# Delta rule: inverses woven with half projections and operands, output rows reordered; up and gate products with a 512-wide operand

## What is computed

```python
def squared_relu_mlp(h, w_up, w_down):          # hidden 4096, two layers, first one for both sequences
    return jnp.square(jax.nn.relu(h @ w_up)) @ w_down

def _swiglu(h, w_in, w_out):                    # hidden 2816, twice
    gu = h @ w_in
    return (jax.nn.silu(gu[..., :FFN_HIDDEN]) * gu[..., FFN_HIDDEN:]) @ w_out

def _gated_deltanet(h, w_in, conv_w, a_log, dt_bias, norm_w, w_out):
    proj = h @ w_in
    qkv = jax.nn.silu(_causal_depthwise_conv(proj[..., :n_qkv], conv_w))
    z = proj[..., n_qkv:n_qkv + GDN_V_WIDTH].reshape(b, s, GDN_HEADS, GDN_DV)
    ...
    o = _chunk_gated_delta_rule(q, k, v, g, beta)
    o = o * lax.rsqrt(jnp.mean(o * o, axis=-1, keepdims=True) + RMS_EPS)
    o = o * norm_w.astype(jnp.float32) * jax.nn.silu(z.astype(jnp.float32))
    return o.astype(h.dtype).reshape(b, s, GDN_V_WIDTH) @ w_out

def _chunk_gated_delta_rule(q, k, v, g, beta):
    a_mat = jnp.where(strict, kk * beta[..., :, None] * decay, 0.0) + jnp.eye(c, dtype=jnp.float32)
    sol = lax.linalg.triangular_solve(a_mat, rhs, left_side=True, lower=True, unit_diagonal=True)
    ...
```

## Time and profile before

| | |
|---|---|
| median of 3 runs | 2090.27 us (2086.32 to 2092.71) |
| profiled execution | 2091.75 us, span 2089.9 us |
| TensorE busy | 1898.4 us (91%), 12225 products |
| VectorE busy | 1118.6 us (54%) |
| ScalarE busy | 914.0 us (44%) |
| GpSimd busy | 346.9 us (17%) |
| HBM traffic | 153 GB/s over the span |
| mean granted TensorE clock | 0.941 of full speed |

### The profile page before, as it was taken

The page is one execution under the profiler, slowest core; times in us unless marked ns, Lnnn a source line. Parts: engine busy times, 40 slices in busy tenths (PEclk is TensorE's granted clock), DMA queues, the critical chain, the costliest instruction groups (busy, mean ns, idle before and its releaser), DMA issues.

```text
span 2089.9 us, 29077 instructions
## 1 busy us (share of the span) xinstructions
PE 1898.4 (91%) x12225; PEld 1636.4 (78%) x12225; DVE 1118.6 (54%) x1555; ACT 914.0 (44%) x1419; POOL 346.9 (17%) x396
## 2 busy tenths in 40 slices
PE   4879887999999999968799989998799999999999
PEld 2666656888887887756598969898699978768997
DVE  1555556555575544566455557833445455565554
ACT  2543344344455444634354447532344344444443
POOL 2120112211141121120211130130200005200000
PEclk8899988999999999989899989998999999999999
DMA  8353553445555766421645544310355545504553
GB/s 278 126 201 126 196 178 109 152 146 189 188 170 182 241 212 227 128 82 39 189 151 193 183 142 132 108 64 1 106 170 179 181 167 175 177 1 141 182 190 133
DMA packets 217966, 320.61 MB, mean 153 GB/s; under 512 B 8550, under 2 KB 123946, under 8 KB 217452
## 3 DMA queue, kind: packets, MB, share of 16 engines
q1 hardware_dynamic: 212628, 308.96, 45.5%
q0 software_dynamic: 1744, 6.03, 0.8%
q10 hardware_dynamic: 3464, 3.75, 0.6%
HBM read 317.68 MB, written 1.05 MB: 153 GB/s over the span
## 4 chain that ended last, share of the span: by engine, by line
PE 77%; DVE 9%; ACT 6%; DMA 4%; POOL 2%; issue 2%; SPq 0%; POOLq 0%; ACTq 0%; DVEq 0%
PE ps L69 74%; PE ps L77 3%; DVE WLO L86 3%; DMA RAW<-in_w_mod_dram 1%; ACT WHI L80 1%; DMA RAW<-in_w_in_dram 1%; DVE AR L86 1%; ACT AR L80 1%; POOL SM L86 1%; DMA RAW<-in_w_up_dram 1%; DVE SM L99 1%; ACT XR L80 1%; DVE PMD L86 1%; POOL XR L86 1%; ACT PMD L80 1%
## 5 line engine op out<-in xcount | busy, mean ns | idle before, releaser
L86 DVE TENSOR_TENSOR WLO<-RAW,WHI 128x1024 fp32r<-128x1024 f32 (+2 forms) x504 | 593.6, 1219 | 430.0 <-ACT WHI L80 429.9
L80 ACT ACTIVATE WHI<-RAW 128x1024 fp32r<-128x1024 f32 (+2 forms) x504 | 488.1, 1017 | 416.2 <-PE ps L69 305.6
L69 PE MATMUL ps<-TH,WHI 128*128 128x256 f32 x1664 | 481.6, 289 | 13.2 <-DVE TL L86 10.9
L69 PE MATMUL ps<-TL,WHI 128*128 128x256 f32 x1664 | 476.9, 287 | 0.0
L69 PE MATMUL ps<-TH,WLO 128*128 128x256 f32 x1664 | 476.4, 286 | 0.0
L69 PE MATMUL ps<-WHI,ARR 128*128 128x512 f32 x1120 | 355.8, 394 | 6.1 <-DVE ARR L86 3.1
L69 PEld LDWEIGHTS ps<-TH,WHI 128*128 128x128 f32 x1664 | 325.6, 196 | 23.9 <-issue 13.5
L69 PEld LDWEIGHTS ps<-TL,WHI 128*128 128x128 f32 x1664 | 325.8, 196 | 0.2
L69 PEld LDWEIGHTS ps<-TH,WLO 128*128 128x128 f32 x1664 | 325.5, 196 | 0.0
L69 PE MATMUL ps<-WHI,TH 128*128 128x512 f32 (+2 forms) x608 | 240.9, 396 | 23.3 <-DVE WLO L86 22.7
L69 PEld LDWEIGHTS ps<-WHI,ARR 128*128 128x128 f32 x1120 | 211.0, 188 | 57.2 <-issue 9.3
(11 more groups left out here) (193 smaller groups left out, 1957.1 us busy)
## 6 DMA issues: line engine op xcount, KB each, us to landing
RAW<-in_w_mod_dram SPq DMA_DIRECT2D x48, 1024.0 KB, 5.3
RAW<-in_w_up_dram SPq DMA_DIRECT2D x48, 1024.0 KB, 5.4
RAW<-in_w_down_dram SPq DMA_DIRECT2D x48, 1024.0 KB, 5.2
RAW<-in_ffn_w_in_dram SPq DMA_DIRECT2D x44, 1024.0 KB, 5.1
RAW<-in_w_in_dram SPq DMA_DIRECT2D x20, 1024.0 KB, 5.3
RAW<-in_ffn_w_out_dram SPq DMA_DIRECT2D x20, 1024.0 KB, 5.1
RAW<-in_dil_w_in_dram SPq DMA_DIRECT2D x18, 1024.0 KB, 5.1
RAW<-in_gdn_w_in_dram SPq DMA_DIRECT2D x16, 1024.0 KB, 5.6
```

The source lines that it names most:

```text
L69: return Made(None if self.eng is None else self.eng.matmul(o, l, r, start=start, stop=stop))
L80: return Made(None if self.eng is None else self.eng.activation(o, i, f, **k))
L86: return Made(None if self.eng is None else self.eng.tensor_tensor(o, a, b, op))
```

## The change

- A product of a half now has one PSUM bank of its own. The moving operand of the high weights is TH and TL together (T2, one tensor TT, two runs of 256 tokens), 512 wide, into both halves of the bank; the low weights with TH go 256 wide into the first half. VectorE then adds the halves (`dve_halves`), a reduction over pairs 256 numbers apart, into SBUF. Relu and Silu now run in place in SBUF. In the feedforward the product of gate and up goes from VectorE to GpSimd (`pool_ffn`) and is rounded one pair later. The convolution projections keep their old form, but hand out a step for each half.
- In the delta rule the convolutions from the eighth on (ALONE = 7) count as two steps each; q's normalisation runs beside the last four, and the operand steps beside the gate's z units from the third. The weave is now 20 steps with 20.
- In the chunks `ring` gets banks 5, 6, 7, 2, 3, 4; outputs 2 and 3 come before the transposes of 0 and 1; GpSimd gates two groups at a time. `pe_gdnout` goes through the first column half token tile by token tile, tile 2 ahead of the transposes of groups 2 and 3; the second weight tile is split before them.

```diff
-        def pe_cols_half(t, b, f, xh, xl, cs, need):
+        def pe_cols_half(key, t, f, nt, cs, need):
             hi, lo = t.of(t.hi), t.of(t.lo)
-            o = b[:, 256 * f:256 * f + 256]
+            fs = slice(128 * f, 128 * f + 128)
+            x2 = T2v(nt)
+            banks.take((key, f), gring)
+            wait_free((key, f))
+            b = banks.of((key, f))
+            both, first = b.rearrange("p (s t) -> p s t", s=2), b[:, 0:256]
             for k in range(8):
                 pe.wait_ge(dve_w, ("lo", t.i, k // 4))
                 need(k)
-                m = pe.matmul3(o, hi[:, k, 128 * f:128 * f + 128], lo[:, k, 128 * f:128 * f + 128], xh[:, k, cs], xl[:, k, cs], k == 0, k == 7)
-            return m
+                if k > 0:
+                    pe.matmul(first, lo[:, k, fs], x2[:, 0, k, cs], False, False)
+                m = pe.matmul(both, hi[:, k, fs], x2[:, :, k, cs], k == 0, k == 7)
+                if k == 0:
+                    pe.matmul(first, lo[:, k, fs], x2[:, 0, k, cs], False, False)
+            m.then_inc(pe_gemm, ("acc", key, f), *([("used", t.i)] if f == 1 else []))
+
+        def dve_halves(signal, o, key, f, *said):
+            b = banks.of((key, f))
+            dve.wait_ge(pe_gemm, ("acc", key, f))
+            dve.reduce(o, b.rearrange("p (s t) -> p t s", s=2), ALU.add).then_inc(signal, ("free", (key, f)), *said)
...
+        def dve_upsum(l, sq, hc, c, f):
+            key, _, _ = up_parts(l, sq, hc, c)
+            wait_tmp(dve, l, sq, key)
+            dve_halves(dve_hd, tmp(l, sq, key)[:, 256 * f:256 * f + 256], ("up", l, sq, hc, c), f, ("sum", key, f))
...
         def pe_rest():
+            qn, ops = pe_l2(0), pe_operands()
             for n, c in enumerate(CONVS):
-                pe_conv(c)
+                for f, _ in enumerate(pe_conv(c)):
+                    if n >= ALONE:
+                        if n > ALONE:
+                            next(qn, None)
+                        yield
...
+            run(qn)
             for c in range(2):
-                for _ in pe_rows(("z", c), z_spec(c), TLS, rows_of("gdn"), normed("gdn")):
-                    next(qn, None)
+                for i, _ in enumerate(pe_rows(("z", c), z_spec(c), TLS, rows_of("gdn"), normed("gdn"))):
+                    if 4 * c + i >= 2:
+                        next(ops)
                     yield
-            yield from qn
-            yield from pe_operands()
+            yield from ops
...
         def pe_chunks():
+            ring.set(5, 6, 7, 2, 3, 4)
+            gring.set(0, 1, 2, 3)
...
             pe_value(3)
+            pe_output(2)
+            pe_output(3)
             pe_outturn(0)
-            pe_output(2)
             pe_outturn(1)
-            pe_output(3)
+
+        def pe_gdnout():
+            g = pe_rows(("go", 0), GDN_OUT[0], TLS, gdn_lhs, gdn_need, apart=True)
+            advance(g, 2)
             pe_outturn(2)
             pe_outturn(3)
+            run(g)
+            run(pe_rows(("go", 1), GDN_OUT[1], TLS, gdn_lhs, gdn_need))
...
-            weave((rest, 22), (inv, 20))
+            weave((rest, 20), (inv, 20))
...
         def act_ffn(l, t):
+            def rounded(c):
+                _, tb, hi, _ = ffn_parts(c)
+                act.wait_ge(pool_hd, ("fm", l, c))
+                act.act(hi, tb, ACT.Copy).then_inc(act_hd, ("fh", l, c))
             for c in range(11):
+                ta = ffn_parts(c)[0]
                 act_splits(tile_of["ffn_w_in_2", l, 0, 256 * c])
+                if c >= 1:
+                    rounded(c - 1)
+                act.wait_ge(dve_hd, ("sum", l, c, 0, 1))
+                act.act(ta, ta, ACT.Silu).then_inc(act_hd, ("fs", l, c))
                 act_splits(tile_of["ffn_w_in_2", l, 0, FFH + 256 * c])
...
         def dve_ffn(l, t):
+            def rest(c):
+                _, tb, hi, lo = ffn_parts(c)
+                dve.wait_ge(act_hd, ("fh", l, c))
+                dve.tt(lo, tb, hi.bitcast(F32), ALU.subtract).then_inc(dve_hd, ("f", l, c))
             for c in range(11):
+                for x, o in enumerate(ffn_parts(c)[0:2]):
+                    dve_splits(tile_of["ffn_w_in_2", l, 0, FFH * x + 256 * c])
+                    if c >= 1 and x == 0:
+                        rest(c - 1)
+                    if c >= 4:
+                        dve.wait_ge(*((pool_hd, ("fm", l, c - 4)) if x == 0 else (dve_hd, ("f", l, c - 4))))
+                    for f in range(2):
+                        dve_halves(dve_hd, o[:, 256 * f:256 * f + 256], ("f", l, c, x), f, ("sum", l, c, x, f))
+            rest(10)
```

More of the change, by code:

```diff
@@ L403, in spec, with row_steps, pe_rows @@
             return [(name, idx, k, min(4, k0 + nk - k), c0, n) for k in range(k0, k0 + nk, 4)]
-        def pe_rows(key, ws, tls, lhs, need, r=gring):
+        def row_steps(ws, tls, apart):
+            steps = [((c, w), ti) for c, w in enumerate(ws) for ti in tls]
+            return sorted(steps, key=lambda s: s[1]) if apart else steps
+        def pe_rows(key, ws, tls, lhs, need, r=gring, apart=False):
             n, nk = ws[0][5], sum(w[3] for w in ws)
-            for c, w in enumerate(ws):
+            for (c, w), ti in row_steps(ws, tls, apart):
@@ new lines, in pe_rows @@
+                o = banks.of((key, ti))[:, 0:n]
+                for k in range(t.nk):
+                    kk = t.k0 - ws[0][2] + k
+                    pe.wait_ge(dve_w, ("lo", t.i, 2 * k // t.nk))
+                    need(kk, ti)
+                    lh, ll = lhs(kk, ti)
+                    m = pe.matmul3(o, lh, ll, hi[:, k, :], lo[:, k, :], kk == 0, kk == nk - 1)
+                said = [("used", t.i)] if ti == tls[-1] else []
+                if c == len(ws) - 1:
+                    said.append(("acc", key, ti))
@@ L2085, in second @@
                 act_square(t, ti, 1, 7)
-            run(act_rows((gkey, 0), specs[0], TLS, first if t else None))
+            run(act_rows((gkey, 0), specs[0], TLS, first if t else None, apart))
             run(act_rows((gkey, 1), specs[1], TLS, second if t else None))
@@ L2625, in dve_rest @@
                     dve_gates_of_rule()
+                if n > ALONE:
+                    next(qn, None)
                 yield
-            qn = dve_l2(0, 128.0)
+            run(qn)
             for c in range(2):
@@ L2631, in dve_rest, with pool_rest @@
                         dve_conv(CONVS[11])
+                    if 4 * c + i >= 2:
+                        next(ops)
+                    yield
+            yield from ops
+        def pool_rest():
+            qn = pool_l2(0)
+            for n in range(12):
+                if n > ALONE:
                     next(qn, None)
+                if n >= ALONE:
                     yield
-            yield from qn
-            yield from dve_operands()
-        def pool_rest():
-            for _ in CONVS:
+                if n > ALONE:
+                    next(qn, None)
                 yield
-            qn = pool_l2(0)
+            run(qn)
             def z(c):
@@ L2649, in pool_rest @@
                 for _ in pool_rows(("z", c), z_spec(c), TLS, z(c)):
-                    next(qn, None)
                     yield
-            yield from qn
-            for _ in range(8):
-                yield
+            yield
+            yield
         S1, VN = NB, TB
@@ L2863, in pe_ffn @@
             for c in range(11):
[L2864 to L2865 removed]
+                for x in range(2):
+                    w = use("ffn_w_in_2", l, 0, 8, FFH * x + 256 * c, 256)
+                    for f in range(2):
+                        pe_cols_half(("f", l, c, x), w, f, 256, slice(0, 256), need)
             def lhs(k, ti):
```

209 lines of the change are left out of this document (104 added, 105 removed).

## The result

The changed kernel takes 2068.85 us (median of 4 runs, 2067.24 to 2070.60) where the kernel before, beside it, takes 2090.90 (4 runs): the ratio is 0.9898, 95% interval 0.988 to 0.9916. That is 22 us less; 2058, 32 us less, was forecast. The profiled executions have spans of 2089.9 and 2068.8 us, 21.1 us apart.

The account below looks back on a forecast made before the run. TensorE was taken to bound feedforwards and the second layer's perceptron, waits and half clock to cost the delta rule's tail; 8.9 + 7.0 + 5 + 11 = 31.9 us off 2091.75 gives 2059.9, as median 2058, range 2045 to 2077.

Parts of the forecast that it names:

- Part 1, the products, feedforwards: Feedforwards: each of 704 blocks takes 0.3475 us instead of 0.360, TensorE stays the bound; 8.9 us less.
- Case A: Products: two runs do not stream as one, so the new form gains nothing; 2076 us, chance 0.07.
- Case D: Feedforward and perceptron tiles: slow sums make VectorE the bound, deciding from about 1.45 us a sum; 2189 us, chance 0.03.
- Part 1, perceptrons: Perceptrons of both layers: cheaper blocks save 9.8 us, less 2.8 for queue and loads; 7.0 us less.
- 2.3 us for VectorE's queue: Perceptrons: deduction because sums delay a queue that also carries attention and gated linear attention; 2.3 us.
- "for the places where a load sets the pace": Perceptrons: deduction where a faster TensorE only waits longer for a load; 0.5 us.
- rival B: Perceptrons: sums in VectorE's queue delay attention's and linear attention's steps, 48 tiles x 0.15 us; 2065 us, chance 0.10.
- "which hides it": Perceptrons: the sum ahead of the split is hidden, as the split waits 1.05 us for its high half anyway.
- Part 2, the inverses: Delta rule up to the value products: fewer waits 2, faster clock 4, table loads against it 1; 5 us less.
- Case C: Delta rule's first part: no gain, as inverse levels wait for VectorE in the convolutions; 2063 to 2068 us, chance 0.16.
- Part 3, first rows early: Delta rule from the value products to the projection's end: outputs follow one another, projection starts earlier; 11 us less.
- Case E: Delta rule's end: late differences behind the weight split stop the projection, early rows give 3 us; 2066 us, chance 0.04.

Follow-up runs that it names:

- e1: Kernel before with the delta rule's part of the change alone, all products in their old form: 2076.17 us, ratio 0.9936.
- e2: Changed kernel with all 48 w_up tiles of the perceptrons back in their old form: 2070.82 us, ratio 0.9904.
- e6: Changed kernel with each sum of the perceptrons made twice on VectorE: 2067.89 us, ratio 0.9898.
- e4: Changed kernel with the perceptrons' sums behind VectorE's residual and weight split of the same step: 2107.86 us, ratio 1.0085.
- e5: Changed kernel with 64 tiny transposes ahead of the first perceptron, moving TensorE's instruction fetches half a piece earlier: 2063.73 us, ratio 0.9879.
- e7: Kernel before with the chunks' part alone (six banks, new order of outputs, `pe_gdnout`), old weave: 2081.20 us, ratio 0.996.
- e8: e3 with the output projection's second weight tile split at the start of the chunks: 2064.08 us, ratio 0.9888.
- e3: Changed kernel with only the first layer's 32 w_up tiles back in their old form: 2064.50 us, ratio 0.9885.
- e11: Changed kernel with 96 tiny transposes ahead of the first perceptron, fetches three quarters of a piece earlier: 2062.41 us, ratio 0.9878.

## Why the prediction was right or wrong

**Part 1, the products, feedforwards: right.** The starts at full clock:

```profile
1545.62 0.40 PE L69 MATMUL ps<-TT,WHI 128*128 128x512 f32 x1
1545.86 0.39 PE L69 MATMUL ps<-TT,WLO 128*128 128x256 f32 x2
1546.08 0.40 PE L69 MATMUL ps<-TT,WHI 128*128 128x512 f32 x1
1546.32 0.28 PE L69 MATMUL ps<-TT,WLO 128*128 128x256 f32 x1
1546.43 0.39 PE L69 MATMUL ps<-TT,WHI 128*128 128x512 f32 x1
1546.66 0.27 PE L69 MATMUL ps<-TT,WLO 128*128 128x256 f32 x1
1546.78 0.40 PE L69 MATMUL ps<-TT,WHI 128*128 128x512 f32 x1
```

From 1546.08 to 1546.78 two blocks take 0.70 us: 0.350 for one, not 0.3475; 0.233 go to the wide product and 0.117 to the narrow. The block gains 0.010 us, not 0.013. For 352 blocks that is 3.5 us, which is what feedforward 1 lost. Feedforward 0's piece shrank by 4.76 us all the same (4.45 forecast), since it has 3.0 us at half clock instead of 5.8, worth 1.4. Both feedforwards together: 8.4 us against 8.9, of which the blocks give 7.0; 6.1 between e1 and e2. Case A (no gain) falls. TensorE was never short of a sum there; VectorE is busy 121 us of 182 (115 forecast), GpSimd's product is hidden.

The Trainium skill (TensorE: Matmul & The Clock Gate, "Wait — 56ns, not 53.3ns?") would give 352 x 2.5 ns = 0.9 us for this piece, an estimate from its page. The blocks gave 3.5; the rows were the better guide.

**Case D: falls with its price.** A sum that reads PSUM numbers 256 apart takes 0.685 us, as a reduction over neighbours does. The Trainium skill (Advanced Engine Details and Errata, "PSUM Cachelines") says that every two consecutive elements in PSUM should be contiguous for best throughput, and that patterns that aren't contiguous slow down matmuls; this sum on VectorE shows no penalty of that kind in its 184 rows. e6 shows for the second layer that the point from which D decides was wrong as well.

**Part 1, perceptrons: the step that failed.** 7.0 us were forecast; the second layer gave 1.9 of its 2.3, and the first took 4.9 where it should have given 4.7. The sum had two terms against the gain, 2.3 us for VectorE's queue and 0.5 us "for the places where a load sets the pace". Neither holds what happened.

The larger is the second: at such a place a load of 5.4 us became one of 7, and half clock followed it. In the profiled executions 6.4 of the 9.6 us hang on where TensorE's fetches fall (537.6 against 531.1 to 531.3 in three kernels that differ only in the dummy transposes). The timed runs show less, 1 to 4 us by the ratios, and don't separate it from nothing for each kernel by itself. The new form didn't make this by being slow; it has fewer instructions, and by that its fetches fall elsewhere. I hadn't looked at DMA's instruction queue at all.

The smaller is VectorE's queue, rival B's mechanism, and where it can be seen it is a few long steps and not 0.15 us for each tile. With the fetches out of the way the third stretch gains 3.9 to 4.2 us (231.3, the mean of the six kernels with the old form other than e1, to 227.4), more than the 2.4 forecast; but they have 4.5 us at half clock there in the mean and the new form 0.6, which leaves about 2. First stretch and gap together lose 2.6 (301.2 to 303.8), where 2.4 less were forecast. The place where the first stretch loses is in ScalarE's queue; in the kernel before, relu comes straight out of PSUM, behind the split:

```profile
355.80 1.99 ACT L80 ACTIVATE WHI<-RAW 128x1024 fp32r<-128x1024 f32 x2
357.70 0.57 ACT L80 ACTIVATE AR<-ps 128x512 f32<-128x512 f32 x1
358.30 0.63 ACT L80 ACTIVATE ARR<-AR 128x512 fp32r<-128x512 f32 x1
```

in the changed kernel it waits for VectorE, which does the linear attention's predicated copies (L105) before it comes to the sum:

```profile
357.28 1.22 DVE L86 TENSOR_TENSOR PMD<-PMD,AR 128x1024 f32<-128x1024 f32 x1
358.42 1.35 DVE L105 COPY_PREDICATED AR<-MU,ps 128x512 f32<-128x512 uint8 x2
359.65 0.68 DVE L99 TENSOR_REDUCE AR<-ps 128x256 f32<-128x512 f32 x1
...
355.38 2.00 ACT L80 ACTIVATE WHI<-RAW 128x1024 fp32r<-128x1024 f32 x2
360.37 0.63 ACT L80 ACTIVATE AR<-AR 128x512 f32<-128x512 f32 x1 [2.99 <-DVE AR L99]
361.03 0.63 ACT L80 ACTIVATE ARR<-AR 128x512 fp32r<-128x512 f32 x1
```

Relu starts 4.99 us after the split instead of 1.90, 3.22 us after it the next time (at 369.31), and TensorE waits 1.2 us for hidden values and 0.9 for a low part, where it waited for neither before. The prediction said that the split waits for its high half anyway, "which hides it"; it looked at what stands behind the sum and not at who waits for it. e4 (39 us, clock included, for one place in the queue) shows how much hangs on that wait, e6 (3.9 us in the first stretch for double the work) that the place weighs more than the length. That all of the 2.6 us come from it is not shown: the gap's 1.4 us go with half clock in the stretch from 593 to 640 (granted 0.96 instead of 1.00), which e5 doesn't have; e5 is 1.7 us longer in the first stretch instead, 1.2 us of it in a longer wait for a low part.

**Part 2, the inverses: right.** 151.0 us against 152, from 156.7. But the gain is the clock's. The waits sum to 12.2 us and to 12.1 before (forecast 13 and 15), so the 2 us taken for them did not come. The granted clock of the kernel before is in the last columns of

```profile
1299.45:1456.19 156.74, 143.34 (x1043) 135.97 (x1041) 88.36 (x177) 61.15 (x125) 28.52 (x19) 0.92 0.19 61
```

Summed from the trace, 26.3 us of this stretch run at half clock before and 14.3 after. That is the prediction's 26 and 14; but 12 us less are worth up to 6, and the sum had 4 for them, 2 for the waits and 1 against for table loads. The wait before the first level came as described, but for GpSimd, whose mask took 7.50 us beside VectorE's:

```profile
1314.40 1.27 POOL L86 TENSOR_TENSOR XN<-AR,CF 128x512 f32<-128x512 f32 x1 [18.09 <-DVE AR L96]
1318.79 7.50 POOL L86 TENSOR_TENSOR XN<-AR,CF 128x512 f32<-128x512 f32 x1 [3.12 <-DVE AR L96]
```

TensorE waited 3.0 us there (3.7 forecast). The table loads rose from 26 to 32. Case C falls.

**Part 3, first rows early: right, 2 us too large, and in part the clock's.** 9.1 us found, 8.4 to 8.9 in e7, 11 taken. Term by term from the value products: products 15.7 us instead of 14.2 (the first 16 at half clock), first projection product at 17.9 instead of 17, two units 7.3 instead of 5.3, then 2.0 and 16.8 instead of 2.1 and 16.3. Most of the 2 us of the units is the split that took 4.17 us beside GpSimd's gates (e8). Case E had the right place, VectorE behind the weight split, and the wrong size. The kernel before has 11.2 us at half clock from the value products to the projection's end, the changed kernel 2.8 and e7 3.9. So up to 4.2 of the 9.1 us are clock; the prediction counted its new order at full clock but for 1 us, and gave no reason for it.

**Sum.** 8.4 + 1.9 - 4.9 + 5.7 + 9.1 = 20.2 of the 21.1 us between the spans; the rest is in stretches that the change doesn't touch (attention 0.8 more, the dilated attention 1.6 less). The time lay inside the range. In part that is luck: the clock gave 2 us more in part 2 and 1.4 in feedforward 0 than the sum had worked out for it, where the waits and the blocks gave less. The delta rule has 51.6 us at half clock before and 30.6 after, worth up to 10.5 of its 14.8, and in e2 and e3, with the same delta rule, 23.3. Case C's 2063 to 2068 came nearest in time with a reason that the runs refute; case B's reason is at most a third of the truth.

## What to carry to other kernels

When a result moves from PSUM into a sum on another engine, follow who read the bank before: its wait now ends behind everything in that engine's queue, and the place of the new instruction in the queue can matter more than its length. Where a chain of load, split and product has no cover, look at every DMA that can share its time, the instruction fetches included, before a gain of a few us is believed or given up. And before code of a few us is kept or dropped, shift it: four places of the fetches here gave 531 us three times and 538 once in the profiled executions, with the same work. Where a stretch got shorter, sum its time at half clock before and after, too: part of a gain can be the clock's.

## What the runs showed of the hardware that I had not expected

TensorE's program arrives in pieces of 16 KB, on DMA queue 8, one for about 256 instructions (85 pieces, 1.39 MB in all, in the changed kernel). A piece that falls into a 1 MB load can make it 1 to 2 us longer: 7.34 and 7.04 us for 5.3 to 5.7, 6.71 in e1. Not every piece does. Of the changed kernel's 1 MB loads that were issued with no other under way, the 125 without such a piece took 4.8 to 5.8 us, the 41 with one 5.1 to 7.3, 19 of them over 6; over all fourteen traces 7 of 1766 without and 163 of 528 with one took over 6 us. The two long loads repeat: in e4, whose TensorE program is the changed kernel's, the same two loads took 7.10 and 7.41 us.

VectorE and GpSimd can stretch each other: 4.17 and 3.52 us together, 2.35 and 2.53 apart, and a mask on GpSimd took 7.50 us instead of 1.27. The Trainium skill (SBUF — State Buffer, "Who interferes with whom") says that a VectorE instruction with two SBUF inputs contends with a GpSimd one that reads SBUF, and calls the shared ports an exclusive lock. The rows agree that they contend. In the first pair both became longer; beside the mask VectorE's split kept its 2.35 us.

The time at half clock (1.2 GHz) in a stretch can differ with the same instructions in it: the same delta rule took 250.6 us in the changed kernel and in e5 and 247.1 in e3. Its place in the span doesn't decide it: between the table's cuts it starts at 1233.7 us in e11 and at 1233.8 in e3, and takes 258.3 and 254.8. What decides it stays open.

Behind TensorE's waits of 2.87 us (up to 643.90) and 2.96 us (up to 763.47) the clock fell to half for 3.4 us each; behind the same two in e5, 1.13 and 1.53 us, it didn't. So loads that came 3.2 us late in all cost 6.4.
